# Three layers of a hybrid network on one core: the order of work in the attention tiles is changed

## The chip, the cores and the metric

The kernel runs on one core of one Trainium2 chip. The metric is the device time of one execution in microseconds (us). A core has a matrix engine (PE, TensorE), a vector engine (DVE, VectorE), a scalar engine (ACT, ScalarE), a general engine (POOL, GpSimd) and a queue that issues the DMAs (SP, SyncE). They run side by side and wait for each other on semaphores only. PE writes to eight PSUM banks of 128 x 512 floats, here two accumulators `acc0` and `acc1` and six others, `bank[0]` to `bank[5]`.

## The reference

A sequence of 512 tokens of width 1024 goes through one block of one kind and two layers of another. What the change touches is in the second kind (`hybrid_layer`), which runs twice. Three mixers (sliding attention, RWKV-7, retention) read the same normalised input; each goes through its own output matrix, is multiplied by a gate, and the three are added:

```python
g = jax.nn.sigmoid(gates).reshape(B, T, N_BRANCH, D)
mixed = g[:, :, 0] * o_a + g[:, :, 1] * o_b + g[:, :, 2] * o_c
x = x + mixed @ w_out
```

The attention has 8 query heads, 2 key heads of width 64, blocks of 128 queries that look at their own block and the one before, and a sink in the denominator:

```python
s = jnp.where(mask[None, :, None, None], s, -jnp.inf)
m = jnp.maximum(jnp.max(s, axis=-1, keepdims=True), sink)
p = jnp.exp(s - m)
p = p / (jnp.sum(p, axis=-1, keepdims=True) + jnp.exp(sink - m))
o = jnp.einsum('bnhgqs,bnshd->bnqhgd', p.astype(v.dtype), vb)
```

All is computed in float32.

## The kernel before

**Slots.** Every weight matrix is cut into slots. A slot is one output chunk of 128 channels for all 512 tokens: 8 blocks of 128 x 128 weights (4 where the input is 512 wide, such as the output of a mixer). To keep float32 precision, weights and inputs are split into a high and a low part, and `slot(s, I, a, chunks)` issues three passes: w_hi x hi, w_hi x lo, w_lo x hi, so 24 matmuls of 128 x 512, or 12. The slots come in pairs: slot 0 of pair I adds into `acc0`, slot 1 into `acc1`. There is one copy of `raw`, `w_hi` and `w_lo` for each of the two. SP loads `raw[s]`; POOL splits it (`split_pair`): it writes `w_hi` (L348) once PE's second pass of the slot before is done (`hi_done`), and `w_lo` (L352) once that slot is all done (`slot_done`); PE's next slot waits for this (`w_split`), and for DVE to have read the accumulator (`acc_free`).

**The stage around the change.** In each layer 24 pairs make the gates and the output projections: slot 0 of a pair is a chunk of the gates' matrix on the normalised input `xg`, slot 1 a chunk of a mixer's output matrix. Pairs 0 to 7 (RWKV's output, `y1`) run between the four tiles of retention, pairs 8 to 15 (retention's output, `y2`) between the four tiles of attention, pairs 16 to 23 (attention's output, again in `y1`) come last in a loop. On DVE `gate(i, O)` multiplies acc0 by `rstd` into `ffn_t` and frees acc0; ACT makes the sigmoid (`gate_sigmoid(i)`, into `ffn_act`); `branch(i, O, dst)` multiplies acc1 by it and frees acc1; `add_branch(k)` is such a branch and a sum into `mixed`.

**One tile of attention** (n = 0 to 3), by engine, in the order of its queue:

- PE: `slot(0, F)`, `slot(1, F)`, `slot(0, F + 1)`, transposes of the probabilities (L1039, two halves of four heads, each after its `pn`), `slot(1, F + 1)`, wait for `pTe`, the products with V into `bank[4]`, then `attend(n + 1)`: the scores of the next tile into banks 0 to 3. Behind the last tile PE waits for `s4["done"]` and enters the loop of pairs 16 to 23.
- DVE: two copies into `an_v` (V of this and the last block), wait for the scores, then for each half mask, maxima, and `an_nm`, `an_es` (L1822 to L1830); `gate(DC + 2n)`; for each half the sum, reciprocal and product with it (`an_s`, 128 x 1024); `add_branch(0)`, `gate(DC + 2n + 1)`, `add_branch(1)`; wait for the products with V; copy to `an_o` (L1846), cast to `y_hi`, difference to `y_lo`; `done`.
- ACT: for each half the exponentials with their sums; load of the sigmoid's table; the two gates' sigmoids, the second of which waits for DVE's `gate(DC + 2n + 1)`; then the four evictions of the transposed probabilities to `an_pT`, and `pTe`.
- POOL and SP: nothing but the splits and the loads of the pairs.

The order within each engine is written out by hand. `bass` helpers such as `tt` and `splitted` record all their operations under lines 1073 and 1080; `mm` under line 473.

Of the kernel before, what the change touches and what calls it, by code (L numbers as in the profile page):

```python
# [18 lines left out]
P = 128  # L19
T = 512  # L20
NT = T // P
D = 1024
DC = D // P
# [84 lines left out]
def build(nc, dram, out):  # L108
    ctx = ExitStack()
    with ctx:  # L110
# [58 lines left out]
        y1_hi, _ = place("y1_hi", (4, T), F32R, offset=rw_at)  # L169
        y1_lo, _ = place("y1_lo", (4, T), F32R, offset=rw_at + C4)  # L170
        z_at, _ = place("z_at", (6, T), offset=rw_at + 2 * C4)
# [41 lines left out]
        an = {}  # L213
# [13 lines left out]
        bank = [ctx.enter_context(nc.psum_tensor(f"bank{s}", [P, T], F32)) for s in range(6)]  # L227


        def sem(name):  # L230
# [26 lines left out]
        s4 = {n: sem("an_" + n) for n in (  # L257
            "sq", "ss", "root", "kn", "kc", "sc", "mx", "p", "pn", "pT", "pTe", "o", "done")}
# [11 lines left out]
        def r3(ap, k):  # L270
            return ap.rearrange("p (a b) -> p a b", a=k)
# [4 lines left out]
        def tile_of(t, a, k, n):  # L276

            return t[:, a:a + k, bass.ts(n, P)]
# [5 lines left out]
        def _(sp):  # L284
# [12 lines left out]
            for name, _ in KEEP[:-1]:  # L297
                sp.dma_start(K[name][:], dram[name]).then_inc(keep_in, 16)
            I = 0
            for c in range(DC):  # L300
# [166 lines left out]
        def _(pe):  # L467
# [87 lines left out]
            xg, hid, yy, em = (xg_hi, xg_lo), (hid_hi, hid_lo), (y_hi, y_lo), (emb_hi, emb_lo)  # L555
            y1, y2, four = (y1_hi, y1_lo), (y2_hi, y2_lo), range(4)
            full = range(DC)
# [68 lines left out]
            for lev in range(8):  # L626
# [28 lines left out]
                if lev == KH_LEV:  # L655
# [3 lines left out]
                    for n in range(NT - 1):  # L659
                        for j in range(2):  # L660
                            o = bank[4 + n // 2][:, (2 * (n % 2) + j) * P:(2 * (n % 2) + j + 1) * P]
# [38 lines left out]
            I = feed_forward(B1_IN + 2 * X_OUT, 0, DC, 2, 10)  # L700
# [8 lines left out]
            with pe.Fori(0, LAYERS) as l:  # L709
                I = B1_PAIRS + l * LAYER_PAIRS  # L710

                def after(name, j, k, per):

                    pe.wait_ge(s2[name], l * 4 * per + j * per + k)
                    pe.sem_inc(pe_turn, 1)
# [208 lines left out]
                I = I + RW_PAIRS  # L924
                for j in range(4):
                    rwkv_pair(j)
                I = I + RET_PAIRS
# [16 lines left out]
                I = I + AT_PAIRS  # L944
# [13 lines left out]
                O = I  # L958
# [17 lines left out]
                def attend(n):  # L976

                    after(s4, "kc", n)
                    for j in range(4):
                        for p in range(2):  # L980
                            r = slice(p * HD, (p + 1) * HD)
                            last = mm(bank[2 * p + j // 2][:, (j % 2) * 2 * P:(j % 2 + 1) * 2 * P], z_at[r, j, n * P:(n + 1) * P],
                                      an["k"][r, j // 2, n * P:(n + 2) * P], True, True)
                    last.then_inc(s4["sc"], 1)
# [4 lines left out]
                for n in range(NT):  # L989
# [18 lines left out]
                    for h in range(8):  # L1008
                        j, p = h // 2, h % 2
# [15 lines left out]
                I = O + 2 * NT  # L1025

                for n in range(NT):
                    F = I + 2 * n
                    slot(0, F, xg, full)
                    if n == 0:  # L1030
                        pe.wait_ge(s3["done"], l * NT + NT)
                        pe.sem_inc(pe_turn, 1)
                    slot(1, F, y2, four)
                    slot(0, F + 1, xg, full)
                    for p in range(2):
                        after(s4, "pn", n, p + 1, 2)
                        for j in range(4):
                            for b in range(2):
                                last = nc.tensor.transpose(bank[2 * p + j // 2][:, (2 * (j % 2) + b) * P:(2 * (j % 2) + b + 1) * P],  # L1039
                                                           an["s"][:, p, j, b * P:(b + 1) * P], K["ident"][:])  # L1040
                        last.then_inc(s4["pT"], 1)
                    slot(1, F + 1, y2, four)
                    after(s4, "pTe", n)
                    for h in range(8):
                        j, p = h // 2, h % 2
                        kv = h // 4
                        for b in range(2):
                            last = mm(bank[4][p * HD:(p + 1) * HD, j * P:(j + 1) * P], an["v"][:, b, kv * HD:(kv + 1) * HD],
                                      an["pT"][:, 4 * p + j, b, :], b == 0, b == 1)
                    last.then_inc(s4["o"], 1)  # L1050
                    if n < NT - 1:
                        attend(n + 1)

                I = I + 2 * NT
                pe.wait_ge(s4["done"], l * NT + NT)
                pe.sem_inc(pe_turn, 1)
                with pe.Fori(0, DC) as j:
                    slot(0, I + j, xg, full)
                    slot(1, I + j, y1, four)
                I = I + DC  # L1060
# [6 lines left out]
        def _(dve):  # L1067
            v = nc.vector
# [9 lines left out]
            def splitted(hi, lo, src):  # L1078

                v.tensor_copy(hi, src)  # L1080
                dve.drain()
                return tt(lo, src, bits(hi), ALU.subtract)
# [324 lines left out]
            I, pre = B1_IN + 2 * X_OUT, 0  # L1407
            fw = vec[:, U_FW:U_FW + 6 * FFC].rearrange("p (i s k) -> p i s k", s=2, k=3)
            fb = vec[:, U_FB:U_FB + 2 * FFC].rearrange("p (i s) -> p i s", s=2)
            for k, n in enumerate(PARTS):  # L1410
# [23 lines left out]
                I, pre = I + n, pre + n  # L1434
# [58 lines left out]
            with dve.Fori(0, LAYERS) as l:  # L1493
                I = B1_PAIRS + l * LAYER_PAIRS
# [17 lines left out]
                def after(name, j, k, per):  # L1512
                    dve.wait_ge(s2[name], l * 4 * per + j * per + k)

                def say(name, k=1):
                    dve.drain()
                    dve.sem_inc(s2[name], k)
# [174 lines left out]
                I = I + RW_PAIRS  # L1692
# [3 lines left out]
                I = I + RET_PAIRS  # L1696
# [22 lines left out]
                I = I + AT_PAIRS  # L1719

                def gate(i, first):

                    scaled(0, first + i, ffn["t"][:]).then_inc(acc_free[0], 1)
                    dve.drain()
                    dve.sem_inc(o_gate, 1)
# [8 lines left out]
                O = I  # L1734
# [67 lines left out]

                ms(an["v"][:])
                dve.drain()
                for n in range(NT):

                    def add_branch(k):
                        j = 2 * n + k
                        branch(DC + j, O, ffn["sq"][:])
                        tt(mixed[:, j, :], mixed[:, j, :], ffn["sq"][:], ALU.add)  # L1810
                        dve.drain()

                    v.tensor_copy(an["v"][:, 0, :], an["v"][:, 1, :])
                    dve.drain()
                    v.tensor_copy(an["v"][:, 1, :], z_at[:, 5, n * P:(n + 1) * P])
                    mask = K["atmask"][:, n, :]

                    after(s4, "sc", n)
                    for p in range(2):
                        hs = slice(4 * p, 4 * p + 4)  # L1820
                        for b in range(2):
                            v.scalar_tensor_tensor(an["s"][:, p, 2 * b:2 * b + 2, :], r3(bank[2 * p + b][:], 2), HD ** -0.5, mid(mask, 2),  # L1822
                                                   ALU.mult, ALU.add)
                        dve.drain()  # L1824
                        v.tensor_reduce(an["mx"][:, hs], an["s"][:, p], AX.X, ALU.max)  # L1825
                        dve.drain()
                        tt(an["mx"][:, hs], an["mx"][:, hs], pcol(V_SINK + 4 * p, 4), ALU.max)
                        dve.drain()
                        v.tensor_scalar(an["nm"][:, hs], an["mx"][:, hs], -1.0, None, ALU.mult)
                        tt(an["es"][:, hs], pcol(V_SINK + 4 * p, 4), an["mx"][:, hs], ALU.subtract)  # L1830
                        say(s4, "mx")
                    gate(DC + 2 * n, O)
                    for p in range(2):
                        hs = slice(4 * p, 4 * p + 4)
                        after(s4, "p", n, p + 1, 2)
                        tt(an["sum"][:, hs], an["sum"][:, hs], an["es"][:, hs], ALU.add)
                        dve.drain()
                        v.reciprocal(an["sum"][:, hs], an["sum"][:, hs])
                        dve.drain()
                        tt(an["s"][:, p], an["s"][:, p], bc(an["sum"][:, hs], 2 * P))  # L1840
                        say(s4, "pn")
                    add_branch(0)
                    gate(DC + 2 * n + 1, O)
                    add_branch(1)
                    after(s4, "o", n)
                    v.tensor_copy(an["o"][:], r3(bank[4][:], 4))  # L1846
                    dve.drain()
                    splitted(tile_of(y1_hi, 0, 4, n), tile_of(y1_lo, 0, 4, n), an["o"][:])
                    say(s4, "done")

                with dve.Fori(0, DC) as j:
                    gate(2 * DC + j, O)
# [4 lines left out]
                I = I + O_PAIRS  # L1857
# [504 lines left out]
```

## Time and profile before

| | us |
|---|---|
| median of 3 runs (lowest, highest) | 2806.37 (2797.89, 2806.93) |
| profiled execution, its own time | 2793.08 |
| its span | 2791.2 |
| PE busy | 2656.3 (95%) |
| DVE, ACT, POOL busy | 1461.8 (52%), 605.0 (22%), 1493.3 (54%) |
| mean granted PE clock | 0.986 |

The attention tiles of the first layer run from 1158.8 to 1254.2 us of the span, those of the second from about 2199 to 2294.6. In the rows, the first number of a line of a timeline is the start in us from the start of the span, the second how long the group took, "x" how many instructions are merged in it, and the bracket the idle time of the engine just before it and what ended that. Matmuls are pipelined, so the time of a group of matmuls reaches a little beyond the start of the next.

### The profile page before, as it was taken

To read this page: it belongs to the slowest core of one execution; us is meant where nothing else is said; L and a number is where in the kernel's file an instruction comes from. 1 tells how busy PE (TensorE), PEld (TensorE's weight loads), DVE (VectorE), ACT (ScalarE), POOL (GpSimd) and SP (SyncE) were. 2 spreads that over 40 slices of the span, in tenths; PEclk is the share of its full clock that TensorE was granted. 3 is DMA by queue.
4 is the path that set the end of the run, shared out by engine and by line. 5 is a ranking of instruction groups with operands and counts; after the bars stand their busy time and mean duration, and the time that the engine had idled before them with its cause. 6 is when DMAs were issued, how large, how long until landed. Compare 5 with 4: busy or idle time off the path is not lost.

```text
span 2791.2 us, 47735 instructions
## 1 busy us (share of the span) xinstructions
PE 2656.3 (95%) x16442; PEld 2071.4 (74%) x16442; DVE 1461.8 (52%) x2081; ACT 605.0 (22%) x1087; POOL 1493.3 (54%) x977
## 2 busy tenths in 40 slices
PE   7878999998999999999999999999999999999999
PEld 5656888876776667777788887776667777788887
DVE  5766737364555646774342524456637764442424
ACT  2323000023223313440200002223313440200002
POOL 4554665665544443445666666644444436666665
PEclk9989999999999999999999999999999999999999
DMA  4212333323211121222333333311121122333333
GB/s 145 69 31 83 92 97 90 98 81 105 83 47 47 47 71 57 69 68 83 92 96 91 98 90 110 92 54 46 40 78 57 61 69 90 93 95 92 97 91 98
DMA packets 72727, 222.69 MB, mean 80 GB/s; under 512 B 9344, under 2 KB 12544, under 8 KB 72576
## 3 DMA queue, kind: packets, MB, share of 16 engines
q1 hardware_dynamic: 72576, 220.63, 26.0%
q8 instruction: 100, 1.64, 0.2%
q14 instruction: 51, 0.42, 0.0%
HBM read 218.50 MB, written 2.10 MB: 79 GB/s over the span
## 4 chain that ended last, share of the span: by engine, by line
PE 87%; DVE 6%; issue 3%; DVEq 2%; DMA 1%; POOL 1%; ACT 1%; SPq 0%; ACTq 0%; POOLq 0%
PE acc L473 75%; PE bank L473 11%; DVE an_mx L1825 1%; DMA raw<-in_w_pg 1%; PE bank L1039 1%; DVE an_mx L1073 0%; POOL w_lo L352 0%; DVE mixed L1073 0%; DVE an_s L1822 0%; DVEq L1824 0%; DVE y_lo L1073 0%; DVE rw_Lr L1531 0%; DVE ffn_sq L1073 0%; DMA x<-in_x 0%; DVE ffn_t L1073 0%
## 5 line engine op out<-in xcount | busy, mean ns | idle before, releaser
L352 POOL TENSOR_TENSOR w_lo<-raw,w_hi 128x1024 fp32r<-128x1024 f32 (+3 forms) x438 | 959.1, 2190 | 308.5 <-PE acc L473 292.5
L348 POOL TENSOR_SCALAR w_hi<-raw 128x1024 fp32r<-128x1024 f32 (+3 forms) x438 | 429.4, 980 | 802.3 <-PE acc L473 656.2
L473 PE MATMUL acc<-xg_hi,w_hi 128*128 128x512 f32 x2224 | 606.9, 410 | 55.6 <-issue 16.4
L473 PE MATMUL acc<-xg_lo,w_hi 128*128 128x512 f32 x2224 | 587.3, 399 | 0.0
L473 PE MATMUL acc<-xg_hi,w_lo 128*128 128x512 f32 x2224 | 586.1, 398 | 0.0
L473 PEld LDWEIGHTS acc<-xg_hi,w_hi 128*128 128x128 f32 x2224 | 418.4, 191 | 181.4 <-issue 87.7
L473 PEld LDWEIGHTS acc<-xg_lo,w_hi 128*128 128x128 f32 x2224 | 418.3, 189 | 101.1 <-issue 0.9
L473 PEld LDWEIGHTS acc<-xg_hi,w_lo 128*128 128x128 f32 x2224 | 415.9, 188 | 101.4 <-issue 1.0
L1870 ACT ACTIVATE ffn_act<-ffn_t 128x512 f32<-128x512 f32 x100 | 63.3, 633 | 811.5 <-DVEq L1133 619.5
L1073 DVE TENSOR_TENSOR x<-x,acc 128x512 f32<-128x512 f32 x104 | 71.3, 688 | 318.8 <-PE acc L473 318.3
L473 PE MATMUL acc<-hid_hi,w_hi 128*128 128x512 f32 x656 | 182.8, 396 | 3.7 <-POOL w_lo L352 1.6
L473 PE MATMUL acc<-hid_hi,w_lo 128*128 128x512 f32 x656 | 182.1, 395 | 0.0
L473 PE MATMUL acc<-hid_lo,w_hi 128*128 128x512 f32 x656 | 181.9, 395 | 0.0
L473 PEld LDWEIGHTS acc<-hid_hi,w_hi 128*128 128x128 f32 x656 | 123.1, 188 | 37.4 <-issue 6.8
L473 PEld LDWEIGHTS acc<-hid_hi,w_lo 128*128 128x128 f32 x656 | 123.1, 188 | 30.0
L473 PEld LDWEIGHTS acc<-hid_lo,w_hi 128*128 128x128 f32 x656 | 123.2, 188 | 29.3
L1073 DVE TENSOR_TENSOR ffn_sq<-acc,rstd 128x512 f32<-128x512 f32 x44 | 30.4, 691 | 212.4 <-PE acc L473 212.4
L1073 DVE TENSOR_TENSOR ffn_t<-acc,rstd 128x512 f32<-128x512 f32 x100 | 69.1, 691 | 136.4 <-PE acc L473 119.1
L1887 ACT ACT_TABLE_LOAD x96 | 123.2, 1283 | 5.3 <-issue 2.7
L1073 DVE TENSOR_TENSOR ffn_h<-ffn_act,ffn_sq 128x512 f32<-128x512 f32 x44 | 94.1, 2139 | 13.4 <-issue 13.4
L432 POOL TENSOR_TENSOR rw_TL<-rw_SCB,lev 64x256 f32<-64x256 f32 (+2 forms) x72 | 65.7, 912 | 54.1 <-PE bank L473 43.2
L473 PE MATMUL acc<-y_hi,w_hi 128*128 128x512 f32 x256 | 75.9, 417 | 17.5 <-issue 9.9
(341 smaller groups left out, 2764.9 us busy)
## 6 DMA issues: line engine op xcount, KB each, us to landing
raw<-in_w_up SPq DMA_DIRECT2D x132, 512.0 KB, 3.6
raw<-in_w_down SPq DMA_DIRECT2D x48, 512.0 KB, 3.6
raw<-in_w_gate SPq DMA_DIRECT2D x48, 512.0 KB, 3.6
raw<-in_w_ret SPq DMA_DIRECT2D x32, 512.0 KB, 3.6
raw<-in_w_rw SPq DMA_DIRECT2D x28, 512.0 KB, 3.6
raw<-in_w_o SPq DMA_DIRECT2D x48, 256.0 KB, 2.6
raw<-in_w_in SPq DMA_DIRECT2D x18, 512.0 KB, 3.6
raw<-in_w_down SPq DMA_DIRECT2D x24, 384.0 KB, 3.0
```

The lines of the kernel that those rows point to most:

```text
L348: nc.gpsimd.tensor_scalar(w_hi[:, s, 0:n], raw[:, s, 0:n], 1.0, 0.0, ALU.mult, ALU.add).then_inc(w_half[s], 1)
L352: nc.gpsimd.tensor_tensor(w_lo[:, s, 0:n], raw[:, s, 0:n], bits(w_hi[:, s, 0:n]), ALU.subtract).then_inc(w_split[s], 1)
L432: nc.gpsimd.tensor_tensor(rw["TL"][to, lev % 2].rearrange("p h n t -> p (h n) t")[:, lo:hi, :], tl[frm, lo:hi, :], K["lev"][frm, lev:lev + ...
L473: return nc.tensor.matmul(o, a, b, start=first, stop=last, skip_group_check=shared)
L1039: last = nc.tensor.transpose(bank[2 * p + j // 2][:, (2 * (j % 2) + b) * P:(2 * (j % 2) + b + 1) * P], an["s"][:, p, j, b * P:(b + 1) * P] ...
L1073: return v.tensor_tensor(o, a, b, op)
L1825: v.tensor_reduce(an["mx"][:, hs], an["s"][:, p], AX.X, ALU.max)
L1870: return nc.scalar.activation(o, i, f, **kw)
L1887: nc.scalar.preload_act_table_set(name)
```

## The change

On PE the scores of the next tile are issued ahead of the products with V. On DVE the eviction of a tile's output becomes `attended(n)`. It is called in the next tile, behind that tile's maxima and its first gate, and once behind the loop for the last tile; the two copies into `an_v` move behind it. In tile 0 the first gate stands between the two halves of the maxima. Behind the last tile, PE issues the first slot 0 of the last eight pairs ahead of the wait for `done`, the first slot 1 behind it, and the loop does the other seven pairs.

```diff
@@ PE, in the tile n
                     slot(1, F + 1, y2, four)
                     after(s4, "pTe", n)
+                    if n < NT - 1:
+                        attend(n + 1)
                     for h in range(8):
...
                     last.then_inc(s4["o"], 1)
-                    if n < NT - 1:
-                        attend(n + 1)

                 I = I + 2 * NT
+                slot(0, I, xg, full)
                 pe.wait_ge(s4["done"], l * NT + NT)
                 pe.sem_inc(pe_turn, 1)
-                with pe.Fori(0, DC) as j:
+                slot(1, I, y1, four)
+                with pe.Fori(1, DC) as j:
                     slot(0, I + j, xg, full)
                     slot(1, I + j, y1, four)
@@ DVE
+                def attended(n):
+
+                    after(s4, "o", n)
+                    v.tensor_copy(an["o"][:], r3(bank[4][:], 4))
+                    dve.drain()
+                    splitted(tile_of(y1_hi, 0, 4, n), tile_of(y1_lo, 0, 4, n), an["o"][:])
+                    say(s4, "done")
+
                 for n in range(NT):
...
-                    v.tensor_copy(an["v"][:, 0, :], an["v"][:, 1, :])
-                    dve.drain()
-                    v.tensor_copy(an["v"][:, 1, :], z_at[:, 5, n * P:(n + 1) * P])
                     mask = K["atmask"][:, n, :]
...
                         say(s4, "mx")
-                    gate(DC + 2 * n, O)
+                        if n == 0 and p == 0:
+                            gate(DC, O)
+                    if n > 0:
+                        gate(DC + 2 * n, O)
+                        attended(n - 1)
+                    v.tensor_copy(an["v"][:, 0, :], an["v"][:, 1, :])
+                    dve.drain()
+                    v.tensor_copy(an["v"][:, 1, :], z_at[:, 5, n * P:(n + 1) * P])
                     for p in range(2):
...
                     add_branch(1)
-                    after(s4, "o", n)
-                    v.tensor_copy(an["o"][:], r3(bank[4][:], 4))
-                    dve.drain()
-                    splitted(tile_of(y1_hi, 0, 4, n), tile_of(y1_lo, 0, 4, n), an["o"][:])
-                    say(s4, "done")
+                attended(NT - 1)
```

## Rows read from the trace of the kernel before

**Rows 1.** The page, busy us of PE and its weight loads, share, instructions.

```profile
PE 2656.3 (95%) x16442; PEld 2071.4 (74%) x16442; DVE 1461.8 (52%) x2081; ACT 605.0 (22%) x1087; POOL 1493.3 (54%) x977
```

**Rows 2.** Waits of PE, 1150 to 1260 us: total us, times, longest.

```profile
PE acc L473 <- DVE ffn_t L1073: 6.0, 4, 1.5
```

**Rows 3.** Timeline of PE: before the tiles, tile 1, behind tile 3.

```profile
1055.11 2.05 PE L473 MATMUL bank<-an_sq,headones 128*128 128x512 f32 x2 [2.24 <-DVEq L1715]
...
1179.18 2.02 PE L473 MATMUL bank<-an_pT,an_v 128*64 128x128 f32 x32
1181.13 2.00 PE L473 MATMUL bank<-an_k,z_at 64*128 64x256 f32 x16
...
1188.77 1.10 PE L473 MATMUL acc<-y_hi,w_hi 128*128 128x512 f32 x4
...
1193.23 2.10 PE L473 MATMUL acc<-xg_hi,w_hi 128*128 128x512 f32 x8 [1.49 <-DVE ffn_t L1073]
...
1198.90 1.91 PE L1039 MATMUL bank<-ident,an_s 128*128 128x128 f32 x16
1200.56 1.18 PE L473 MATMUL acc<-y_hi,w_hi 128*128 128x512 f32 x4
...
1203.53 2.02 PE L473 MATMUL bank<-an_pT,an_v 128*64 128x128 f32 x32
...
1257.01 3.40 PE L473 MATMUL acc<-xg_hi,w_hi 128*128 128x512 f32 x8 [2.77 <-DVEq L1743]
```

**Rows 4.** Busy time by window: from tile 1's first slot to tile 2's; behind tile 3.

```profile
1183.06:1207.41 24.35, 22.86 (x138) 18.31 (x137) 17.98 (x30) 10.13 (x26) 10.65 (x8) 1.00 0.23 65
...
1257.00:1260.30 3.30, 3.29 (x9) 2.65 (x10) 0.00 (x0) 0.00 (x0) 0.00 (x0) 0.57 0.00 0
```

The columns of rows 4: window, its length, busy us of PE, weight loads, DVE, ACT and POOL (instructions in brackets), the granted clock as a share of full speed, the DMAs' busy share, GB/s.

**Rows 5.** Timeline of POOL, tile 1.

```profile
1187.25 1.05 POOL L348 TENSOR_SCALAR w_hi<-raw 128x1024 fp32r<-128x1024 f32 x1 [6.48 <-PE acc L473]
1189.18 2.41 POOL L352 TENSOR_TENSOR w_lo<-raw,w_hi 128x1024 fp32r<-128x1024 f32 x1 [0.88 <-PE acc L473]
1191.54 0.63 POOL L348 TENSOR_SCALAR w_hi<-raw 128x512 fp32r<-128x512 f32 x1
1192.34 1.27 POOL L352 TENSOR_TENSOR w_lo<-raw,w_hi 128x512 fp32r<-128x512 f32 x1 [0.16 <-issue]
```

**Rows 6.** Timeline of DVE, tile 1.

```profile
1181.39 0.69 DVE L1846 COPY an_o<-bank 128x512 f32<-128x512 f32 x1
1182.16 0.43 DVE L1080 CAST y_hi<-an_o 128x512 fp32r<-128x512 f32 x1
1182.66 0.69 DVE L1073 TENSOR_TENSOR y_lo<-an_o,y_hi 128x512 fp32r<-128x512 f32 x1
1183.47 0.23 DVE L1813 COPY an_v<-an_v 128x128 f32<-128x128 f32 x1
...
1183.91 1.28 DVE L1822 SCALAR_TENSOR_TENSOR an_s<-bank,atmask 128x512 f32<-128x512 f32 x2
...
1189.81 1.80 DVE L1073 TENSOR_TENSOR an_mx<-an_mx,vec 128x4 f32<-128x4 f32 x1
...
1192.44 0.69 DVE L1073 TENSOR_TENSOR ffn_t<-acc,rstd 128x512 f32<-128x512 f32 x1 [0.19 <-issue]
...
1195.87 1.22 DVE L1073 TENSOR_TENSOR an_s<-an_s,an_sum 128x1024 f32<-128x1024 f32 x1
...
1199.12 0.69 DVE L1073 TENSOR_TENSOR ffn_t<-acc,rstd 128x512 f32<-128x512 f32 x1
```

**Rows 7.** Timelines of POOL and DVE, a place in the first block.

```profile
127.99 3.15 POOL L352 TENSOR_TENSOR w_lo<-raw,w_hi 128x1024 fp32r<-128x1024 f32 x1 [0.17 <-issue]
...
129.01 2.41 DVE L1080 CAST y_hi<-m_tg 128x512 fp32r<-128x512 f32 x1
```

**Rows 8.** Timeline of ACT, tile 1: the evictions of the transposed probabilities.

```profile
1200.52 2.05 ACT L1870 ACTIVATE an_pT<-bank 128x512 f32<-128x512 f32 x4
```

**Rows 9.** The page, issues of DMAs: count, KB each, us to landing.

```profile
raw<-in_w_gate SPq DMA_DIRECT2D x48, 512.0 KB, 3.6
```

## The prediction

> **What bounds the kernel now.** I read the page's busy line first: TensorE (PE) is busy 95% of the span [rows 1], so a change counts only through the instants in which PE stands still or runs slow. The waits of PE in the attention stage of the first layer come next: it waits four times, once a tile, 1.5 us each, for VectorE's (DVE) `ffn_t` [rows 2]. That is `slot(0, F + 1)` waiting for acc0, which DVE frees in `gate(DC + 2n)` behind the whole chain of maxima. The fifth wait is 2.77 us before the slot behind `wait_ge(s4["done"])`, and the slot's first 8 matmuls then take 3.40 us instead of 2.10, at a granted clock of 0.57, so mostly on the lower of its two levels [rows 3, 4]. PE's waits here are thus 4 x 1.5 + 2.77, with 1.3 of slow clock on top, 10.1 us a layer, 20 us in both (layer two repeats the pattern). That is the most that the change can win, 0.7%.
>
> **Inside a tile.** I put PE, DVE, GpSimd (POOL) and ScalarE of tile 1 side by side and look at which wait would end next. Two facts matter.
> First, POOL splits the weights of the *next* slot only when this slot's matmuls are done. `slot(0, F)` ends at 1188.77, POOL's `w_lo` starts 0.41 later and ends at 1191.59 [rows 3, 5]; PE has by then just finished `slot(1, F)` (3 x 0.94 from 1188.77). So POOL's splits sit at fixed places relative to PE.
> Second, DVE operations that read two SBUF operands, or copy from SBUF to SBUF, don't run beside POOL's. `an_mx` of 128x4, 0.16 us when alone, took 1.80 us from 1189.81 and ended with POOL's `w_lo` (1189.18 + 2.41) [rows 5, 6]; a cast that takes 0.43 alone took 2.41, and ended 0.28 after POOL's `w_lo` [rows 6, 7]. From these I use: the later one ends at (end of the other) - 0.14 + its own duration, and one that waits goes before one that comes later. `ffn_t<-acc,rstd` at 1192.44, with a PSUM operand, ran its 0.69 beside POOL's `w_lo` of 1192.34 [rows 5, 6].
>
> **The change part by part.** Let t = 0 be the start of `attend(n)`, the scores. PE then has scores 1.93, products with V 1.95, `slot(0, F)` 3.88 to 9.59, `slot(1, F)` to 12.41 (the slot started at 1183.06, as the window does) [rows 3, 4]; the sum is the same in either order.
> (a) *Scores first.* DVE gets the scores at 2.15 instead of 4.73 (in the old order copies of V and the eviction also stood before them). The maxima then run their 5.90 to `an_mx` of the second half, 8.05, where POOL's `w_hi` (1187.25, so 8.07 to 9.12) holds them until 9.1 or so. All are out by 9.45. `gate` now waits for PE's `slot(0, F)` instead: 9.59 + 0.19 = 9.78, done 10.47. So acc0 is free before `slot(1, F)` ends and the 1.5 us go. What is late next is `w_lo`, 10.00 to 12.40, plus 0.24 to PE: `slot(0, F + 1)` starts at 12.65, against 14.05 before: 1.40 won, for the moment.
> (b) *Output of the last tile behind `gate`, copies of V behind it.* Same five operations: 0.69 + 0.43 + 0.69 + 2 x 0.23 [rows 6]. They used to run at 2.2 to 4.8, where POOL is idle; they now run exactly beside POOL's `w_lo`, `w_hi`, `w_lo`. Copy from PSUM 10.68 to 11.37; cast asked 11.45, held by `w_lo` until 12.40, ends 12.69; POOL's `w_hi` (0.63) gets in, ends 13.17; `y_lo` ends 13.72; POOL's second `w_lo` (1.27) gets in, ends 14.85; first copy of V ends 14.94, second 15.24. Alone they would be done at 13.29: 1.95 lost.
> (c) *Normalisation.* First half 15.15 to 16.88; POOL's next `w_hi` has waited since 16.81 and holds the 128x4 sum until 17.88; the second 128x1024 product runs 18.21 to 19.44 (was: ended 17.91 [rows 6]). `slot(0, F + 1)` ends on PE at 18.32, so POOL asks for `w_lo` at 18.73, waits for the product, and holds 19.44 to 21.70. PE transposes the second half 19.54 to 20.37, 0.4 of standing.
> (d) *`add_branch(0)`, then `gate(DC + 2n + 1)`.* `ffn_sq` 19.70 to 20.39, the sum `mixed` asked 20.47, held by `w_lo`, ends 22.25; the gate 22.40 to 23.09. ScalarE's sigmoid and its four evictions of P transposed come behind this gate: from the start of the gate to their end 3.45 us (1199.12 to 1202.57 [rows 6, 8]), so 25.85, 25.95 at PE. PE's `slot(1, F + 1)`, started at 20.49 when `ffn_sq` has freed acc1, is over 2.97 later [rows 3], at 23.46. **PE then stands 2.3 us in front of `attend(n + 1)`**, a wait that had 0.85 us to spare before (slot over 1203.53, evictions 1202.57, 0.1 to PE [rows 3, 8]). The tile takes 25.95 against 24.35 (1179.18 to 1203.53): 1.60 lost. The DVE operations are the same ones; it is their place against POOL's that costs.
> Tile 0 has no output to evict, but `gate` now stands between its halves, so its second maxima fall beside POOL's splits and come 1.7 later; I cost it like the others, 1.60. Tile 3 ends with V's products behind the same evictions: 1.60 too. Sum 6.4 a layer.
> (e) *One slot ahead of the last wait.* `slot(0, I)` follows V's products at once, 1.95 behind their start, instead of 2.02 + 2.77 = 4.79 [rows 3], and lasts 5.7, while DVE's copy, cast and difference need 2.1 and have no splits beside them. `slot(1, I)` finds `done` set. Won: 2.84, and 1.3 of slow clock [rows 4]: 4.15 a layer. The loop of 8 becomes 1 + 7: nothing that these rows can price, 0.1 at most either way, the registers of one turn.
> No DMA is moved. Each load follows a split: from the end of `w_lo` at 12.40 to the next `w_hi` at 16.81 are 4.4 us, and a gate load lands in 3.6 [rows 9]; 0.8 is left.
> Without the clock: 2 x (6.4 - 4.15) = +4.5 us.
> (f) *The clock.* PE now stands 2.3 us eight times in the run. No such gap stands in the tiles before, so I bound it: the 1.49 us gaps were followed by a granted 1.00 (windows over tile 1 [rows 4]), so 0; the gaps of 2.24 and 2.77 were followed by slow matmuls (two of 128x512 in 2.05; 8 in 3.40 [rows 3, 4]), 1.3 to 1.5 each: at most 8 x 1.45 = 11.6. The new gap is nearest to the 2.24 one; as not every such gap need fall alike, I take five of eight, +7. **Total +11.5 us**: 2804.6 for an execution like the profiled 2793.08, which lay 13.3 under the median of the runs; from that median, 2806.37, I forecast 2818.
>
> **A rule weighed.** The copies of V, 0.227 us in all eight, were never beside POOL's work here, so no row shows them held; the cast of [rows 7] is the nearest. The Trainium skill, SBUF — State Buffer, section "Who interferes with whom", speaks against the change: a `copy` or `cast` can take the port pair that VectorE and GpSimd share, whichever issues first keeps it for its whole instruction, and the other blocks. By that rule the sum stays as above; were it wrong for the copies of V alone, DVE would be about 0.9 earlier, which is the start of the second rival.
>
> **The rivals.**
> 1. *Stalls, hardly any clock.* As above with two falls or fewer: +4.5 to +7.4, no change that can be told. For it: gaps of 1.49 do nothing. Against: 2.24 did. 2811.
> 2. *Faster: the sum `mixed` gets in before POOL's `w_lo`.* If DVE is 1.7 us earlier at the end of the normalisation than I work out (the copies of V not held, POOL's `w_hi` behind the first product), `ffn_sq` and `mixed` run before 18.73. The point that decides is there. Then the evictions end by 23.25, the wait is 0.3 us, and the tile takes 23.35: 1.0 won four times, with 4.15 at the end, 8.2 a layer: 2806.4 - 16.3 = 2790. Against it: four operations in a row are held on my count, none of them closely.
> 3. *Slower still: the second 128x1024 product loses to `w_lo`.* It is ahead by 0.5 us (18.21 against 18.73). If late, it ends at 22.2, the gate starts at 24.1, attend at 27.65: 3.3 a tile, 2 x (13.2 - 4.15) = +18, with the clock +26: 2832.
> 4. *It cancels*: a small gain in the tiles' place of the loss, about -1 to +3 in all: 2807.
>
> **How the numbers follow.** Forecast 0.50; rival 1 0.17; rival 2 0.17; rival 3 0.10; rival 4 0.06. A difference of 0.3%, 8.4 us, is about what can be told from no change. Slower by more: forecast (nearly all of it, some 0.47) and rival 3: 0.57. Faster: 0.17. Same: 0.26. The range leaves out most of rival 2 and what of rival 3 lies beyond its point: 2796 to 2832; the forecast's own is 2811 to 2826.
>
> **What would show it.** Per tile: `slot(0, F + 1)` right behind `slot(1, F)` with no wait for `ffn_t` (step a); `y_hi` and `an_v` longer than 0.43 and 0.23 (step b); `mixed` of about 1.8 us (d); a PE wait of some 2.3 us before the scores, ended by ScalarE's evictions, and a tile of 25.9 us; the granted clock below 1.00 behind some of these; no wait before the slot on `y1` (e). I am wrong if the scores start without a wait, and so `mixed` ran before POOL's `w_lo`.

## The result and the profile after

The changed kernel takes 2812.62 us (median of 9 runs) beside 2803.4 for the kernel before (9 runs). The ratio is 1.0051, 95% interval 1.0034 to 1.0067: slower by 14.3 us (9.5 to 18.8). This ratio is not that of the two medians, which lie 9.2 us apart. The profiled execution took 2813.38 us, its span is 2811.6, 20.4 more than before.

The first view is the waits of PE from 1158 to 1285 us of the changed kernel, the first layer's tiles: total us, times, longest. The line of [rows 2] is gone, and so is the wait for `done`; in their place PE waits four times for ScalarE's evictions (the first line) and a little for the second half of the probabilities in front of their transposes (the second).

```profile
PE bank L473 <- ACT an_pT L1881: 10.2, 4, 2.6
PE bank L1039 <- DVEq L1745: 1.2, 4, 0.5
```

Timeline of PE in tile 1 and behind tile 3, which answers to [rows 3]. The reader is to see that `slot(0, F + 1)` at 1199.20 has no bracket any more, that the scores (`an_k`) wait 2.58 us and then take 3.55 instead of 2.00, and that the slot at 1271.25 follows V's products at once.

```profile
1185.02 3.21 PE L473 MATMUL bank<-an_k,z_at 64*128 64x256 f32 x16 [2.58 <-ACT an_pT L1881]
...
1190.53 2.13 PE L473 MATMUL acc<-xg_hi,w_hi 128*128 128x512 f32 x8
...
1199.20 2.11 PE L473 MATMUL acc<-xg_hi,w_hi 128*128 128x512 f32 x8
...
1206.17 1.06 PE L1039 MATMUL bank<-ident,an_s 128*128 128x128 f32 x8 [0.26 <-DVEq L1745]
1207.05 1.17 PE L473 MATMUL acc<-y_hi,w_hi 128*128 128x512 f32 x4
...
1212.67 3.55 PE L473 MATMUL bank<-an_k,z_at 64*128 64x256 f32 x16 [2.58 <-ACT an_pT L1881]
...
1267.81 3.51 PE L473 MATMUL bank<-an_pT,an_v 128*64 128x128 f32 x32 [2.44 <-ACT an_pT L1881]
1271.25 2.13 PE L473 MATMUL acc<-xg_hi,w_hi 128*128 128x512 f32 x8
```

DVE in the same tile, beside [rows 6]. The cast takes 1.31 instead of 0.43, the first copy of V 1.12 instead of 0.23, the sum into `mixed` 1.75 instead of 0.84.

```profile
1196.44 0.69 DVE L1075 TENSOR_TENSOR ffn_t<-acc,rstd 128x512 f32<-128x512 f32 x1 [1.79 <-PE acc L473]
1197.26 0.69 DVE L1811 COPY an_o<-bank 128x512 f32<-128x512 f32 x1
1198.03 1.31 DVE L1082 CAST y_hi<-an_o 128x512 fp32r<-128x512 f32 x1
1199.42 0.94 DVE L1075 TENSOR_TENSOR y_lo<-an_o,y_hi 128x512 fp32r<-128x512 f32 x1
1200.48 1.12 DVE L1845 COPY an_v<-an_v 128x128 f32<-128x128 f32 x1
...
1204.77 1.23 DVE L1075 TENSOR_TENSOR an_s<-an_s,an_sum 128x1024 f32<-128x1024 f32 x1
...
1207.04 1.75 DVE L1075 TENSOR_TENSOR mixed<-mixed,ffn_sq 128x512 f32<-128x512 f32 x1
1208.93 0.69 DVE L1075 TENSOR_TENSOR ffn_t<-acc,rstd 128x512 f32<-128x512 f32 x1
```

The same sum in the kernel before, where POOL's `w_lo` came only at 1199.32:

```profile
1198.13 0.84 DVE L1073 TENSOR_TENSOR mixed<-mixed,ffn_sq 128x512 f32<-128x512 f32 x1
```

POOL's splits there, beside [rows 5]: the first `w_lo` (1196.65 to 1199.06) covers the cast, the second the copy of V; the third, asked at 1205.30, waits for DVE's product until 1206.00 and then holds `mixed` until 1208.24.

```profile
1196.65 2.41 POOL L352 TENSOR_TENSOR w_lo<-raw,w_hi 128x1024 fp32r<-128x1024 f32 x1 [0.88 <-PE acc L473]
1199.03 0.80 POOL L348 TENSOR_SCALAR w_hi<-raw 128x512 fp32r<-128x512 f32 x1
1199.99 1.52 POOL L352 TENSOR_TENSOR w_lo<-raw,w_hi 128x512 fp32r<-128x512 f32 x1 [0.16 <-issue]
...
1205.30 2.94 POOL L352 TENSOR_TENSOR w_lo<-raw,w_hi 128x1024 fp32r<-128x1024 f32 x1 [0.86 <-PE acc L473]
```

ScalarE's evictions behind that gate, beside [rows 8], and the windows over the tile and over its slow scores, beside [rows 4]: the granted clock is 0.94 over the tile and 0.54 in the second.

```profile
1210.33 2.04 ACT L1881 ACTIVATE an_pT<-bank 128x512 f32<-128x512 f32 x4
```

```profile
1185.02:1212.67 27.65, 24.82 (x137) 19.73 (x137) 19.14 (x29) 10.13 (x27) 11.65 (x8) 0.94 0.19 57
1212.67:1216.10 3.43, 3.43 (x16) 2.73 (x16) 0.00 (x0) 1.00 (x1) 0.00 (x0) 0.54 0.32 81
```

A measure that the noise of the rest of the kernel doesn't touch is the stage in the profiles: from the start of `attend(0)` to the second slot 0 of the last eight pairs, both layers added. Before it is 1153.95 to 1267.03 and 2194.34 to 2307.64, together 226.38; after, 1157.95 to 1280.01 and 2206.24 to 2327.99, 243.81: +17.4. The other 3.0 of the two spans' difference lie outside the stage, where the program is the same.

The table has the same measure for the changed kernel and for the ten variants of the experiments. Each ratio is to runs of the kernel before taken beside it.

| kernel | stage, both layers, us | against before, us | ratio of runs (95%) |
|---|---|---|---|
| changed | 243.81 | +17.4 | 1.0051 (1.0034 to 1.0067) |
| e1 one slot ahead only | 217.94 | -8.4 | 0.9971 (0.9957 to 0.9985) |
| e2 tiles only | 252.27 | +25.9 | 1.0090 (1.0065 to 1.0116) |
| e3 fill | 231.14 | +4.8 | 1.0013 (1.0000 to 1.0026) |
| e4 sum late | 216.64 | -9.7 | 0.9967 (0.9945 to 0.9990) |
| e5 eviction from PSUM | 223.33 | -3.1 | 0.9984 (0.9969 to 0.9999) |
| e6 no copies of V | 231.31 | +4.9 | 1.0008 (0.9998 to 1.0019) |
| e7 both savings | 215.53 | -10.9 | 0.9948 (0.9930 to 0.9967) |
| e8 both, old order | 214.94 | -11.4 | 0.9962 (0.9946 to 0.9979) |
| e9 both, sum late | 208.57 | -17.8 | 0.9939 (0.9922 to 0.9956) |
| e10 both, first gate behind | 209.48 | -16.9 | 0.9947 (0.9931 to 0.9963) |

0.1% is 2.8 us. Divided by 2803, the stage's difference lies inside the interval of the runs in every line, so the stage explains what was timed.

### The profile page after: what moved, and what is told of

Same layout as the page of the kernel before. It is cut to its first block, busy times and chain, and to the rows that moved or that the text cites. A ratio compares the mean times of both kernels' runs of the same rounds, so it can differ in the third digit from the quotient of the medians.

```text
span 2811.6 us, 47729 instructions
## 1 busy us (share of the span) xinstructions
PE 2671.4 (95%) x16442; PEld 2082.7 (74%) x16442; DVE 1477.9 (53%) x2081; ACT 605.0 (22%) x1087; POOL 1500.9 (53%) x977
## 4 chain that ended last, share of the span: by engine, by line
PE 86%; DVE 6%; issue 3%; DVEq 1%; ACT 1%; DMA 1%; POOL 1%; ACTq 0%; SPq 0%; POOLq 0%
PE acc L473 73%; PE bank L473 12%; DVE an_s L1075 1%; ACT an_pT L1881 1%; DVE mixed L1075 1%; POOL w_lo L352 1%; DMA raw<-in_w_pg 1%; DVE ffn_t L1075 0%; DVE y_hi L1082 0%; DVE y_lo L1075 0%; DVE rw_Lr L1533 0%; DVE ffn_sq L1075 0%; DMA x<-in_x 0%; DVE an_v L1845 0%; DVE an_sum L1075 0%
```

## The experiments

**e1 and e2, the two parts apart.** The kernel before with the last part alone:

```diff
                 I = I + 2 * NT
+                slot(0, I, xg, full)
                 pe.wait_ge(s4["done"], l * NT + NT)
                 pe.sem_inc(pe_turn, 1)
-                with pe.Fori(0, DC) as j:
+                slot(1, I, y1, four)
+                with pe.Fori(1, DC) as j:
```

> The kernel before with only one part of the change: the first slot 0 of the last eight pairs ahead of the wait for done, slot 1 behind it, the loop with seven pairs. My theory: this part alone takes away the 2.77 us wait and the slow clock behind it in each layer, 2 x (2.8 + 1.3 to 1.5) = 8.3 us less than before (ratio 0.997); tiles stay at 24.35 us with four waits of 1.5 for ffn_t. Rival (it brings nothing, DVE's eviction only moves the wait in front of slot 1): within 1 us of before, with a wait of over 1 us before the slot on y1.

And the changed kernel with these lines taken back:

> The change without its last part: scores ahead of V's products and the late eviction stay, the last eight pairs are again one loop behind the wait for done. My theory: the tiles are what costs, 27.65 against 24.35 us each in the changed kernel's profile, eight of them: +26 us against before, and some 8 us slower than the changed kernel. Rival (the tiles are about even and the last part is what costs): within 5 us of before.

Measured: -8.4 us and +25.9 us in the stage. Their sum, +17.5, is the whole. In e1, PE behind tile 3, where the slot follows V's products without a bracket:

```profile
1252.66 2.02 PE L473 MATMUL bank<-an_pT,an_v 128*64 128x128 f32 x32
1254.61 2.13 PE L473 MATMUL acc<-xg_hi,w_hi 128*128 128x512 f32 x8
```

e2 has the wait for `done` again, 2.6 us. Both rivals are out.

**e3, the clock alone.** PE works where it stood: two products that nobody reads are put into the wait.

```diff
                     slot(1, F + 1, y2, four)
+                    for _ in range(2):
+                        mm(bank[5][:], K["ident"][:], z_at[:, 0, :], True, True)
                     after(s4, "pTe", n)
```

> The changed kernel with two idle products of 128x512 (identity times z_at, about 0.95 us each, into bank 5 that nobody reads there) in front of the wait for pTe, so that PE works through most of the 2.58 us for which it stands. The evictions are not touched. My theory: the wait itself stays (the scores start at the same point behind the gate, with 0.6 us of standing left), but the clock stays up: scores and products with V take 3.9 instead of 5.5 us, the tile 26.1 instead of 27.65, 8 x 1.5 = 12 us less than the changed kernel, still about 2 us or more slower than before. Rival (the slow matmuls behind the wait have nothing to do with PE having stood): no change, or 8 x 0.1 slower.

Measured: the stage is 12.7 us shorter than the changed kernel's. PE in front of tile 1, with 0.86 us of standing left, and in front of tile 2 ("x12" and "x4" are parts of the 16 scores, cut by the edge of the view; all 16 take 2.00 us both times; the two products stand as four records):

```profile
1185.94 1.88 PE L473 MATMUL bank<-z_at,ident 128*128 128x512 f32 x4
1188.68 1.57 PE L473 MATMUL bank<-an_k,z_at 64*128 64x256 f32 x12 [0.86 <-ACT an_pT L1883]
```

```profile
1214.66 0.70 PE L473 MATMUL bank<-an_k,z_at 64*128 64x256 f32 x4 [0.86 <-ACT an_pT L1883]
```

The tile is 25.98 us (1188.68 to 1214.66), 1.63 over the 24.35 of before: that is what the later evictions cost by themselves. The changed kernel's 27.65 has 1.67 of slow clock on top. The evictions come no earlier here, only the standing is filled. So the slow matmuls come of PE having stood.

**e4, one operation out of the way of the second gate.** DVE does the same work; only the sum into `mixed` and the gate change places.

```diff
                         branch(DC + j, O, ffn["sq"][:])
+                        if k == 0:
+                            gate(DC + 2 * n + 1, O)
                         tt(mixed[:, j, :], mixed[:, j, :], ffn["sq"][:], ALU.add)
...
                     add_branch(0)
-                    gate(DC + 2 * n + 1, O)
                     add_branch(1)
```

> The changed kernel with one edit on DVE: the sum into mixed of add_branch(0) runs behind gate(DC+2n+1) instead of ahead of it, so POOL's w_lo no longer holds that gate. My theory: the gate starts at 20.6 instead of 22.5 from the start of the scores, the evictions end at 24.1, PE stands 0.5 instead of 2.58 us before the scores and the clock stays up; tile 24.1 to 24.3 us, 8 x 3.4 = 27 us less than the changed kernel, some 8 us less than before. Rival (the evictions wait for something else, as the transposes or the exponentials): the 2.58 us wait stays, time as the changed kernel.

Measured: -9.7 us against before, -27.2 against the changed kernel. DVE and PE in tile 1: the gate now stands ahead of the sum, which is the one that is held (0.86). The wait is 0.75 and the tile 24.16 (1180.16 to 1204.32).

```profile
1199.73 0.69 DVE L1075 TENSOR_TENSOR ffn_sq<-acc,ffn_act 128x512 f32<-128x512 f32 x1 [0.26 <-issue]
1200.59 0.69 DVE L1075 TENSOR_TENSOR ffn_t<-acc,rstd 128x512 f32<-128x512 f32 x1 [0.16 <-issue]
1201.41 0.86 DVE L1075 TENSOR_TENSOR mixed<-mixed,ffn_sq 128x512 f32<-128x512 f32 x1
```

```profile
1180.16 2.00 PE L473 MATMUL bank<-an_k,z_at 64*128 64x256 f32 x16 [0.76 <-ACT an_pT L1882]
...
1204.32 2.00 PE L473 MATMUL bank<-an_k,z_at 64*128 64x256 f32 x16 [0.75 <-ACT an_pT L1882]
```

This decides between the amount of DVE's work and its place: the amount is the same, and all of the tiles' loss is gone.

**e5, e6 and e7, less of DVE's work beside POOL.**

```diff
                 def attended(n):
...
-                    v.tensor_copy(an["o"][:], r3(bank[4][:], 4))
-                    dve.drain()
-                    splitted(tile_of(y1_hi, 0, 4, n), tile_of(y1_lo, 0, 4, n), an["o"][:])
+                    splitted(tile_of(y1_hi, 0, 4, n), tile_of(y1_lo, 0, 4, n), r3(bank[4][:], 4))
```

> The changed kernel, but the eviction reads bank 4 in PSUM twice (cast to y_hi, then the difference to y_lo) in place of copying it to an_o in SBUF first. No operation of the eviction then has two SBUF operands or copies from SBUF to SBUF, so none should be held by POOL's splits, and one of 0.69 us is gone. My theory: y_lo ends at 12.1 from the start of the scores instead of 13.9, the normalisation at 17.4, the sum into mixed comes at 18.5 and so just ahead of POOL's w_lo (18.7), the second gate at 19.3, the evictions of P transposed end at 22.8: the 2.58 us wait goes, the tile takes 22.9 to 23.1 us; 8 x 4.6 = 37 us less than the changed kernel, 19 us less than before (ratio 0.993). Should mixed come behind w_lo after all (0.2 us decide), the wait is about 2 and only 5 us are won against the changed kernel. Rival (the place beside POOL doesn't matter, only the amount of DVE's work): DVE is 0.69 us shorter a tile, so 8 x 0.7 = 6 us less than the changed kernel.

```diff
-                    v.tensor_copy(an["v"][:, 0, :], an["v"][:, 1, :])
-                    dve.drain()
-                    v.tensor_copy(an["v"][:, 1, :], z_at[:, 5, n * P:(n + 1) * P])
...
+                            at_v = (n - 1 + b) * P + kv * HD
+                            vb = z_at[:, 5, at_v:at_v + HD] if n + b > 0 else an["v"][:, 0, kv * HD:(kv + 1) * HD]
-                            last = mm(bank[4][p * HD:(p + 1) * HD, j * P:(j + 1) * P], an["v"][:, b, kv * HD:(kv + 1) * HD],
+                            last = mm(bank[4][p * HD:(p + 1) * HD, j * P:(j + 1) * P], vb,
```

> The changed kernel without the two copies of V in each tile: PE reads V of both blocks where it lies, in z_at. My theory: 1.12 + 0.23 us go in which the first copy is mostly held by POOL's w_lo (0.23 alone), but the normalisation then meets POOL's next w_hi instead, the sum into mixed stays behind w_lo; the second gate comes 0.5 us earlier, the wait before the scores is 2.0 to 2.1 instead of 2.58, tile 27.1; 4 us less than the changed kernel. Rival (DVE's work alone counts, wherever it is): 1.35 us a tile, 11 us less, and no clock loss once the wait is near 1.2: up to 23 us less.

> Both together: eviction from PSUM, no copies of V, the order of the changed kernel. My theory: the second gate is ready before PE needs its evictions by about 0.8 us, whatever POOL does, so nothing is left but POOL's own w_lo in front of slot(0, F+1): tile 22.9 to 23.0 us, the same as the eviction from PSUM alone if mixed got in there, with 19 us less than before (ratio 0.993). Rival (something else is late next, such as the exponentials): tile above 23.5.

e5 won 20.5 us of the stage against the changed kernel, not the 37 expected and not the rival's 6. In layer one tile 1 went as worked out: `mixed` at 1202.33 just ahead of the `w_lo` of 1202.49. In tile 2 it lost the race that I had put at 0.2 us: it was held, took 1.75, and the wait of 2.57 was back. Two views, DVE and POOL:

```profile
1202.33 0.69 DVE L1075 TENSOR_TENSOR mixed<-mixed,ffn_sq 128x512 f32<-128x512 f32 x1
...
1226.77 1.75 DVE L1075 TENSOR_TENSOR mixed<-mixed,ffn_sq 128x512 f32<-128x512 f32 x1
```

```profile
1202.49 2.78 POOL L352 TENSOR_TENSOR w_lo<-raw,w_hi 128x1024 fp32r<-128x1024 f32 x1 [0.29 <-PE acc L473]
...
1225.54 2.43 POOL L352 TENSOR_TENSOR w_lo<-raw,w_hi 128x1024 fp32r<-128x1024 f32 x1 [0.89 <-PE acc L473]
```

And tile 0, which has no output to evict, kept its 2.58, which the expectation left out. e6 won 12.5 against the changed kernel where I expected 4. Its tile 1 is 27.09 (1180.72 to 1207.81), the 27.1 expected, but not by a shorter wait: that stayed 2.57 and not 2.0 to 2.1, and the 0.5 us were won ahead of it, in front of the second half of the transposes. Tile 2 took 25.67, with a wait of 1.12. There, in both layers, a gate load landed 4.8 us after its issue (4.6 in layer two), where it had 4.4 by the prediction (3.6 and 0.8 to spare), and with it the splits that hold DVE were late, so that `mixed` (1228.91) got in ahead of `w_lo` (1228.94):

```profile
1227.13 1.65 POOL L348 TENSOR_SCALAR w_hi<-raw 128x1024 fp32r<-128x1024 f32 x1 [2.74 <-DMA raw<-in_w_gate]
```

Why that load was slow is open. The clock did the rest: it stayed up behind the wait of 1.12, and also behind the wait of 2.43 in front of tile 3's products with V, in both layers (1.99 us for these products, 3.51 in the changed kernel). So the size of e6 missed for two reasons outside both theories, and its total doesn't decide between them. Tile 1, which neither reason touches, does: it lost 0.56 us, where the rival needs 1.35. In e7 tiles 2 and 3 are 22.89 and 22.86 us with no wait at all, as expected, with only POOL's `w_lo` in front of `slot(0, F + 1)`. Tile 0 keeps its wait of 2.58 and tile 1 starts with the slow clock behind it (24.49), so the stage won 10.9 against before and not 19.

```profile
1207.93 2.00 PE L473 MATMUL bank<-an_k,z_at 64*128 64x256 f32 x16
...
1230.82 2.00 PE L473 MATMUL bank<-an_k,z_at 64*128 64x256 f32 x16
...
1253.68 2.02 PE L473 MATMUL bank<-an_pT,z_at 128*64 128x128 f32 x32
```

**e8, the old order with the same two savings.** The edits of e1, e5 and e6 on the kernel before.

> The order of the kernel before in the tiles (V's products ahead of the scores, eviction ahead of the maxima), with the same two savings (eviction from PSUM, no copies of V) and the one slot ahead of the last wait. It says what the new order is worth once DVE has less to do. My theory: the scores come at 4.06 from the start of V's products, the second an_mx at 9.96, level with POOL's w_lo (10.0), so an_mx or an_nm is held until 12.4, the gate starts at 12.7 and PE still waits 0.9 to 1.4 us for ffn_t: tile 23.6 to 24.1 us, 8.3 + 8 x 0.5 = 12 us less than before (ratio 0.996), and 6 us slower than the new order with the same savings. Rival (the order is worth nothing): the same time as the new order with both savings.

Measured: -11.4 us in the stage, tile 23.77 us (1203.98 to 1227.75), the wait for `ffn_t` 0.91:

```profile
1215.49 2.10 PE L473 MATMUL acc<-xg_hi,w_hi 128*128 128x512 f32 x8 [0.91 <-DVE ffn_t L1077]
```

The 12 us less than before came; the 6 us slower than e7 did not. e8 is level with e7 in all, as the rival says, but by two amounts that cancel in each layer: the new order wins 0.9 in each of tiles 1 to 3, 2.7, and loses as much in tile 0 (26.85 against 25.48 us, and the slow clock behind it).

**e9 and e10, tile 0.** e9 is e7 with e4's edit. e10 is e7 with the first gate of tile 0 behind both halves of the maxima:

```diff
-                        if n == 0 and p == 0:
-                            gate(DC, O)
+                    gate(DC + 2 * n, O)
                     if n > 0:
-                        gate(DC + 2 * n, O)
                         attended(n - 1)
```

> The kernel with both savings (eviction from PSUM, V read in z_at) and in addition the sum into mixed behind the second gate. In the kernel with both savings alone only tile 0 of each layer still waits, 2.58 us before the scores, with 1.5 us of slow clock behind it, because its second half of maxima comes behind the first gate. My theory: here too the sum into mixed, held 1.75 us by POOL's w_lo in front of the gate, makes that wait; without it tile 0 waits 0.8 us and the clock stays up: 2 x 3.3 = 6.6 us less than with both savings alone, 21 us less than before (ratio 0.9925). Rival (tile 0 waits for its exponentials or transposes): no change against the kernel with both savings.

> The kernel with both savings, but in tile 0 the first gate stands behind both halves of the maxima, as in the other tiles and as in the kernel before, not between them. My theory: tile 0 then has again the wait for ffn_t of about 1.5 us that it had before, and loses the 2.58 us before the scores and the slow clock: 2 x (4.1 - 1.4) = 5.4 us less than with both savings alone, 20 us less than before (ratio 0.993). Rival (the place of this gate is what keeps tile 0 from losing more): slower than with both savings alone, both waits are there.

Measured: -17.8 and -16.9 us against before in the stage, 7.0 and 6.1 less than e7 where 6.6 and 5.4 were expected. PE in e9 and then in e10, in tile 0: these are the only waits left in the stage that hang on one of DVE's gates, 0.76 and 1.76 us.

```profile
1181.87 2.00 PE L473 MATMUL bank<-an_k,z_at 64*128 64x256 f32 x16 [0.76 <-ACT an_pT L1879]
```

```profile
1166.40 2.11 PE L473 MATMUL acc<-xg_hi,w_hi 128*128 128x512 f32 x8 [1.76 <-DVE ffn_t L1077]
```

Both theories held. e9 at 2776.84 us beside 2794.54 (ratio 0.9939) beats the kernel before, and with it the changed one. e10 against e8 (209.48 to 214.94, 2.7 a layer) is the worth of the new order once DVE is lean: three tiles of 0.9.

## Why the prediction was right

The time, 2812.62, lies in the range of 2796 to 2832 and in the forecast's own 2811 to 2826; the way, slower, was the likeliest, and the forecast of +11.5 stands beside a measured +14.3 (9.5 to 18.8). The difference says more than the time itself, 2812.62 for 2818: the kernel before had a median of 2803.4 over nine runs and not the 2806.37 that the forecast started from. Step by step, with the changed kernel's tile 1 laid on the prediction's scale at `slot(0, F)` (1190.53 = 3.88):

- **(a) The scores first, and the 1.5 us wait goes.** Right: the gate at 1196.44, worked out 9.78, which is 1196.43. `slot(0, F + 1)` starts at 1199.20, worked out 12.65, which is 1199.30. One step inside is off without effect: the second half's `an_mx`, put behind POOL's `w_hi`, was clear of it (0.16 us at 1194.17, `w_hi` at 1194.72), since the slow clock put off the slots by 1.6 us and the maxima by 1.2. In e3, with the clock up, `w_hi` does hold this half: `an_nm` takes 0.96.
- **(b) Five operations beside POOL's splits.** Right within 0.02: cast ends 1199.34 (worked out 1199.34), `y_lo` 1200.36 (1200.37), first copy of V 1201.60 (1201.59). The first copy of V, of which no row showed that it can be held, took 1.12 in place of 0.23. The Trainium skill, SBUF — State Buffer, section "Who interferes with whom", counts a `copy` among the operations that can block each other with GpSimd's; the trace agrees, with that 1.12.
- **(c) The product just ahead of `w_lo`, by 0.5 us.** Right: 1204.77 against 1205.30. Rival 3, which turned on this, did not come; that the tile measured just the 27.65 of this rival is chance, since 1.67 of it is the clock (e3).
- **(d) `mixed` held, the gate late, PE stands before the scores.** Right: the gate at 1208.93 (worked out 1209.05), evictions over at 1212.37 (1212.50), scores at 1212.67 (1212.60). The wait shows as 2.58. The prediction says 2.3, but that is a slip: its own times, 23.46 and 25.95, are 2.49 apart, and its other sums use the times. The tile without the clock is 25.98 in e3, worked out 25.95. That it is the place and not the amount of work is shown by e4.
- **(e) One slot ahead.** Right: 8.4 us in e1, worked out 8.3.
- **(f) The clock.** The one term that was mis-sized: I took five falls of eight. In the profiled execution all eight waits were followed by slow scores or products (3.21 to 3.63 us where 2.0 is full speed), 12.7 us by e3 instead of 7. With eight, the prediction's own bounds give 4.5 + 11.6 = 16.1 for a measured 17.4 in the stage. The count of falls was a choice between two bounds, none and eight, and the upper one came. Not every such wait has it in every kernel: in e5, layer one, the scores behind a wait of 2.57 took 2.00 and V's products 2.02; in layer two, at the same place, they took 2.44 and 3.21. And the kernel before has a wait of 2.24, at 253.95, with no slow matmul behind it, which speaks for rival 1 and which the prediction doesn't weigh.
- **Rivals.** 1 (hardly any clock) and 4 (it cancels) fall with the interval above 1.003. 2 (faster) is out as the case of this kernel, but e5's tiles 1 and 3 and e7's tiles 2 and 3 show its mechanism: with DVE earlier, `mixed` gets in ahead of `w_lo`, no wait is left in front of the next scores, and the tile is 22.9 where the clock is up (e7, and e5's tile 3: 22.90).

**Tile 0.** The prediction names what is particular to it, the first gate between the halves, which puts the second maxima beside POOL's splits, but gives it the price of the others, 1.60. It measured 1.84 (from `attend(0)` to what follows `slot(1, F + 1)`: 1157.95 to 1185.02 = 27.07 us against 1153.95 to 1179.18 = 25.23). That size was close; what was not drawn from it is that this loss has a cause apart from the eviction and so outlives the savings (e7). It goes when that gate is moved (e10) or when the sum no longer stands ahead of the second gate (e9).

## What to carry to other kernels

An operation moved off one wait lands somewhere in the other engines' schedule: lay it beside what shares a resource with it there, and follow the next release behind it, before counting the wait as won. Where two engines exclude each other, what stands ahead of a signal should be what can't be held (one operand in PSUM), and what can be held goes behind it; that cost one call moved here (e4) and turned +17.4 us into -9.7. Split a change into its parts and run each: one half was worth -8.4 us, the other cost +25.9.

## What the hardware showed

Engines here do not wait for each other on semaphores only, as the text ahead of the prediction has it: operations of DVE and POOL also hold each other up where no semaphore stands between them (`mixed` 1.75 in e5's tile 2, 0.69 in its tile 1). Of two engines that exclude each other in this way, the one that waits is served before the other's next operation, so holds alternate: the cast ended at 1199.34, `w_hi` at 1199.83, `y_lo` at 1200.36, `w_lo` at 1201.51, the copy at 1201.60. A held operation ends 0.14 us earlier than the other's end plus its own duration; both engines pay in this way (`w_lo` 2.94 in place of 2.41). In the changed kernel the eight waits of PE of 2.4 to 2.6 us were all followed by a stretch mostly at the lower clock level (granted 0.54 over 3.43 us); those of 1.5 in the kernel before, of 1.8 in tile 0 of e8 and e10, of 1.1 in e6 and of 0.9 in e8 and e3 were not, nor were one of 2.57 in e5 and two of 2.43 in e6. The order of such neighbours can differ between tiles of one execution when it hangs on 0.2 us (e5), and a late load can turn it (e6).
